# A two-layer encoder step with expert retrieval: U blocks and V blocks of the expert mixer in sequence instead of interleaved

## The chip, the cores and the metric

The kernel runs on one core of a Trainium2 chip, as one program. The metric is the device time of that core in microseconds, the median of several runs. Five engines work at once and wait for one another by semaphores: TensorE (PE in the profile), VectorE (DVE), ScalarE (ACT), GpSimd (POOL) and SyncE (SP). SP, ACT and POOL issue DMAs, each on a queue of its own.

## What is computed

One inference step of two layers over 320 tokens (256 prompt rows, 64 sample rows) of width 1024: a token mixer, cross-attention into 256 memory rows, and an expert-retrieval channel mixer, each behind an RMS norm. The change is in the expert mixer, which each of the two layers runs once:

```
q   = (xb @ w_q)                                     # 8 heads, 2 halves of 128
s   = einsum('thpc,hpnc->thpn', q, sub_keys)         # scores against 128 keys a half
...                                                  # top 16 of each half, then of the 256 sums
gate = softmax(top)                                  # 16 chosen experts a head and token
act = gelu(einsum('td,thkd->thk', xb, expert_u[eidx]))
out = einsum('thk,thkd->td', gate * act, expert_v[eidx])
```

There are 16384 experts of width 1024 for u and for v, in float32.

## The kernel before

For the 256 prompt rows the mixer is computed densely: each of 128 **U blocks** multiplies all tokens with 128 experts' u and takes the gelu; a matrix of gate weights, zero for what was not chosen, is multiplied in; each of 128 **V blocks** adds the weighted activations times 128 experts' v into four PSUM banks. For the 64 sample rows the activations come from the same U blocks and go to DRAM (`acts`), and then 64 gathered values and 64 gathered rows of v are accumulated on VectorE (`gather_step`).

All matmul operands are split into a high and a low part (float32r), and three products stand for one.

- **U block** (`split_block`): four quarters. ScalarE makes the high part of a quarter from the raw chunk (`upper_u`, line 1213), GpSimd the low part (`lower_parts`, line 629), TensorE runs 24 matmuls of 320 columns (lines 740 to 742). A quarter's buffer is free again when TensorE has used it. ScalarE takes the gelu (lines 1247, 1248). SP loads chunks of two U blocks, 1 MB, into two buffers; the load of a chunk waits until GpSimd has lowered the chunk before the last.
- **V block** (`v_block`, line 948): VectorE multiplies activations and gate weights (`product`, line 1805), ScalarE makes the high parts of p (line 1310) and v (line 1317), VectorE the low parts (lines 1814, 1816), TensorE runs 12 matmuls of 512 columns. p and v parts have two buffers each; the high parts of block b wait for block b-2. SP loads chunks of two V blocks, 1 MB, into two raw buffers (`v_load`), and the gate weights of 8 blocks, 1 MB, per round (`g_load`).
- **Gathers** (`gather_row`, `gather_act`): GpSimd issues 64 indirect row loads of 0.5 MB and 64 of single values per layer, once all U blocks are lowered. Six row slots.

Order in one layer of the mixer: queries and scores; 32 U blocks (`up`) while VectorE chooses experts; 16 U blocks beside the making of the gate matrix (`gb`), which goes to DRAM; 16 U blocks alone (`ux`); 64 rounds of one U and one V block (`uv`), the V blocks 64 blocks behind; 64 V blocks alone, into which the 64 gathered rows are accumulated. Every engine's program is written out by hand, so the order on a queue is that of the code.

## Time and profile before

| | |
|---|---|
| median of 3 runs | 2702.13 us (2697.93 to 2704.52) |
| the profiled execution | 2692.74 us, span 2690.9 us, mean granted clock of TensorE 0.963 |
| PE busy | 2454.7 us, 91% of the span |
| PE weight loads, DVE, ACT, POOL busy | 2196.0, 1447.4, 1291.1, 1421.7 us |
| HBM read and written | 459.93 and 49.68 MB |
| stages of layer 0 | `up` to 637, `gb` to 737, `ux` to 800, `uv` to 1199, V alone to 1453 us |

Matmuls are pipelined, so TensorE counts as busy while one that has been issued is still on its way; the step from the start of one block to the start of the next tells more than its busy time. Releasers are inferred from semaphores: an idle time is put down to what ended last.

### The profile page before, as it was taken

How to read it: one execution, taken by the hardware profiler on the slowest of the kernel's cores; microseconds unless marked ns; L12 is line 12 of the kernel's file. 1: busy time of each engine (PE TensorE's matmuls, PEld its weight loads, DVE VectorE, ACT ScalarE, POOL GpSimd, SP SyncE). 2: the span in 40 equal slices, each digit the busy share in tenths (PEclk: the TensorE clock that was granted, in tenths of full speed). 3: DMA queues.
4: the chain of work that ended last, by engine and by line, in shares of the span. 5: the costliest groups of instructions: out<-in, count | busy, mean ns of one | idle time of the engine just before them, and what ended most of it. 6: DMA issues, size and time to landing. Idle time of an engine off the chain costs nothing.

```text
span 2690.9 us, 48230 instructions
## 1 busy us (share of the span) xinstructions
PE 2454.7 (91%) x15014; PEld 2196.0 (82%) x15014; DVE 1447.4 (54%) x3071; ACT 1291.1 (48%) x2983; POOL 1421.7 (53%) x1772
## 2 busy tenths in 40 slices
PE   7988899998999999997778899998999999998786
PEld 7877888997999999985556878997999999985564
DVE  2233644898803333337778643898803333337787
ACT  4333534455755555543333434455855555543333
POOL 6634045786584444457721035687675444447731
PEclk9998999999999999999889999999999999999898
DMA  5313423344865564567897422243865555557794
GB/s 189 122 71 134 180 79 110 112 148 145 290 227 192 180 221 176 189 214 254 283 330 284 158 93 103 88 157 131 287 234 187 203 194 186 200 184 263 271 350 175
DMA packets 152660, 510.90 MB, mean 190 GB/s; under 512 B 13601, under 2 KB 89377, under 8 KB 110830
## 3 DMA queue, kind: packets, MB, share of 16 engines
q1 hardware_dynamic: 111662, 383.21, 40.8%
q0 software_dynamic: 31680, 118.06, 11.8%
q10 hardware_dynamic: 9216, 8.39, 0.9%
q8 instruction: 50, 0.82, 0.1%
q14 instruction: 52, 0.43, 0.0%
HBM read 459.93 MB, written 49.68 MB: 189 GB/s over the span
## 4 chain that ended last, share of the span: by engine, by line
PE 56%; POOL 19%; issue 11%; DVE 6%; DMA 5%; ACT 2%; POOLq 1%; DVEq 0%; ACTq 0%; SPq 0%
PE psum L948 14%; POOL w_split L629 12%; PE psum L740 9%; PE psum L741 9%; PE psum L742 9%; PE psum L770 9%; POOL cst L664 5%; DMA w_ring<-peer_v 3%; PE psum L996 2%; POOL w_ring L658 1%; PE psum L932 1%; DVE v_hl L1816 1%; POOL arena L658 1%; DMA w_ring<-peer_v,cst 1%; DVE arena L1376 1%
## 5 line engine op out<-in xcount | busy, mean ns | idle before, releaser
L629 POOL TENSOR_TENSOR w_split<-w_ring,w_split 128x256 fp32r<-128x256 f32 x1152 | 881.4, 771 | 590.5 <-ACT w_split L1213 498.2
L948 PE MATMUL psum<-v_hl,p_hl 128*128 128x512 f32 x3072 | 777.5, 404 | 102.2 <-DVE v_hl L1816 97.8
L740 PE MATMUL psum<-uT_split,w_split 128*128 128x320 f32 x2560 | 813.6, 318 | 20.9 <-POOL w_split L629 8.7
L742 PE MATMUL psum<-uT_split,w_split 128*128 128x320 f32 x2560 | 795.9, 311 | 0.0
L741 PE MATMUL psum<-uT_split,w_split 128*128 128x320 f32 x2560 | 795.8, 311 | 0.0
L948 PEld LDWEIGHTS psum<-v_hl,p_hl 128*128 128x128 f32 x3072 | 582.9, 194 | 260.8 <-issue 145.2
L1213 ACT ACTIVATE w_split<-w_ring 128x256 fp32r<-128x256 f32 x1152 | 480.1, 418 | 652.3 <-PE psum L742 635.8
L740 PEld LDWEIGHTS psum<-uT_split,w_split 128*128 128x128 f32 x2560 | 485.1, 190 | 43.9 <-POOL w_split L629 20.1
L741 PEld LDWEIGHTS psum<-uT_split,w_split 128*128 128x128 f32 x2560 | 485.5, 190 | 4.9
L742 PEld LDWEIGHTS psum<-uT_split,w_split 128*128 128x128 f32 x2560 | 484.8, 189 | 0.0
L1814 DVE TENSOR_TENSOR p_hl<-shared,p_hl 128x256 fp32r<-128x256 f32 x256 | 109.0, 426 | 515.0 <-ACT p_hl L1310 515.0
L1816 DVE TENSOR_TENSOR v_hl<-w_ring,v_hl 128x1024 fp32r<-128x1024 f32 x256 | 314.7, 1229 | 99.2 <-ACT v_hl L1317 98.8
L1107 ACT ACTIVATE w_split<-w_ring 128x256 fp32r (+1 forms) x416 | 171.8, 417 | 269.1 <-PE psum L770 198.5
L424 POOL TENSOR_TENSOR w_split<-w_ring,w_split 128x256 fp32r<-128x256 f32 x296 | 220.6, 750 | 151.6 <-ACT w_split L1107 139.1
L770 PE MATMUL psum<-w_split,uT_split 128*128 128x256 f32 (+1 forms) x2208 | 274.1, 287 | 18.4 <-DVE w_split L424 5.2
L770 PEld LDWEIGHTS psum<-w_split,uT_split 128*128 128x128 f32 (+1 forms) x2208 | 270.4, 183 | 22.5 <-POOL w_split L424 5.8
L1317 ACT ACTIVATE v_hl<-w_ring 128x1024 fp32r<-128x1024 f32 x256 | 268.8, 1050 | 37.0 <-DMA w_ring<-peer_v 36.9
L1310 ACT ACTIVATE p_hl<-shared 128x256 fp32r<-128x256 f32 x256 | 107.2, 419 | 294.0 <-DVE shared L1805 238.5
L1805 DVE TENSOR_TENSOR shared<-arena 128x256 f32<-128x256 f32 (+1 forms) x256 | 108.1, 422 | 112.5 <-issue 112.5
L664 POOL DMA_INDIRECT cst<-acts,cst x128 | 143.8, 1123 | 44.5 <-issue 38.4
L658 POOL DMA_INDIRECT w_ring<-peer_v,cst x84 | 86.4, 1029 | 108.7 <-DVE psum L1735 95.0
L1735 DVE SCALAR_TENSOR_TENSOR psum<-w_ring,cst,psum 128x1024 f32<-128x1024 f32 x84 | 107.7, 1282 | 26.6 <-DMA w_ring<-peer_v,cst 25.8
(260 smaller groups left out, 1874.0 us busy)
## 6 DMA issues: line engine op xcount, KB each, us to landing
w_ring<-peer_u SPq DMA_DIRECT2D x128, 1024.0 KB, 5.0
w_ring<-peer_v SPq DMA_DIRECT2D x128, 1024.0 KB, 6.1
arena<-gates SPq DMA_DIRECT2D x32, 1024.0 KB, 9.8
gates<-w_ring POOLq DMA_DIRECT2D x22, 1024.0 KB, 5.8
w_ring<-w_pq SPq DMA_DIRECT2D x8, 2048.0 KB, 7.7
gates<-arena POOLq DMA_DIRECT2D x10, 1024.0 KB, 8.5
w_ring<-w_qk SPq DMA_DIRECT2D x4, 2048.0 KB, 9.7
w_ring<-w_vo SPq DMA_DIRECT2D x4, 2048.0 KB, 7.9
```

Source lines behind the costliest of these rows:

```text
L424: eng.tensor_tensor(dst, raw, chunk_quarter(name, local, i, q, 0)[1].bitcast(F32), ALU.subtract).then_inc(w_lo_ready, 1)
L629: pool.tensor_tensor(wq[:, q, 1], quarter(raw, m, q), wq[:, q, 0].bitcast(F32), ALU.subtract).then_inc(w_lo_ready, 1)
L664: pool.indirect_dma_start(out=s_val[:, k:k + 1], out_offset=None, in_=acts[l].rearrange("a p (x o) -> (a p x) o", o=1), in_offset=bass.Ind ...
L740: pe.matmul(bank[:, 0:TOK], hi, uT_hi[:, k, :], start=k == 0, stop=False)
L741: pe.matmul(bank[:, 0:TOK], hi, uT_lo[:, k, :], start=False, stop=False)
L742: last = pe.matmul(bank[:, 0:TOK], lo, uT_hi[:, k, :], start=False, stop=k == KD - 1)
L770: last = pe.matmul(out, lhs, rhs, start=r == 0 and a == 0, stop=k == KD - 1 and a == 2, skip_group_check=True)
L948: last = pe.matmul(psum[:, 2 + 2 * t + n, :], lhs, vh[:, part, n * 512:(n + 1) * 512], start=False, stop=False, skip_group_check=True)
L1107: act.activation(dst, raw, ACT.Copy).then_inc(w_hi_ready, 1)
L1213: act.activation(wq[:, q, 0], quarter(raw, m, q), ACT.Copy).then_inc(w_hi_ready, 1)
L1317: act.activation(vhl[:, r % 2, 0, :], v_raw[(r // 2) % 2][:, r % 2, :], ACT.Copy).then_inc(vhi_ready, 1)
L1816: dve.tensor_tensor(vhl[:, r % 2, 1, :], v_raw[(r // 2) % 2][:, r % 2, :], vhl[:, r % 2, 0, :].bitcast(F32), ALU.subtract).then_inc(v_spli ...
```

## The change

All 80 late U blocks now run in one stage (`ur`), and all 128 V blocks after them. The names: EARLY = 48 blocks keep their activations in SBUF, LATE = 80 blocks do not.

- In the `ur` stage VectorE multiplies activations and gate weights in place (`weigh`): one late block at a time in `s_act`, and two early blocks beside each of the first four blocks of rounds 0 to 5. ScalarE stores the weighed late activations by groups of 4 blocks (0.5 MB) to a new DRAM tensor `weighed`, beside the samples' activations.
- SP loads 16 gate chunks in this stage, two of them into a third ring buffer by turns; three gate chunks and the first two V chunks are issued together at the stage's start.
- In the V stage the parts of v have three buffers; the third lies where the U operand was. SP reloads the weighed late activations by 8 blocks (two loads of 0.5 MB).
- The gathered rows have nine slots and are accumulated over blocks 14 to 125, and not over the last 58.
- The memset that clears rows of `u` for the next layer stands behind the wait for the last V block instead of ahead of the copies of the accumulator.

```diff
...
-LAG = 64
+AHEAD = 32
 GB = 16
-XU = 16
-AHEAD = LAG - GB - XU
-UV = (NB - LAG) // 8
+EARLY = AHEAD + GB
+LATE = NB - EARLY
+ROUNDS = LATE // 8
+CATCH = EARLY // 8
 GC = 16
 NGC = NP_ // GC
 PICKS = 64
-SLOTS = 6
+SLOTS = 9
...
-        act4 = view(arena, 0, LAG // 4, 4, NP_)
-        act8 = view(arena, 0, LAG // 8, 8, NP_)
-        g_ring = view(arena, LAG * NP_, 2, NGC, 8 * GC)
-        s_act = view(arena, LAG * NP_ + 4096, 2, 4, NS)
-        spare_rows = LAG * NP_ + 4096 + 512
-        g_stage.append(view(arena, spare_rows, NK // 2, GC, 2))
-        row_slot = [view(arena, spare_rows + h * D, D) for h in range(2)]
-        row_slot += [view(w_ring, s * KD * 512 + h * D, D) for s in range(2) for h in range(2)]
+        act4 = view(arena, 0, EARLY // 4, 4, NP_)
+        p_early = view(arena, 0, EARLY, NP_)
+        g_ring = view(arena, EARLY * NP_, 3, NGC, 8 * GC)
+        g_blocks = g_ring.rearrange("p s c (b t d) -> p s c b t d", t=GC, d=2)
+        p_late = view(arena, EARLY * NP_, 3, 8, NP_)
+        s_act = view(arena, EARLY * NP_ + 6144, 2, 4, TOK)
+        spare_cols = EARLY * NP_ + 6144 + 8 * TOK
+        g_stage.append(view(arena, spare_cols, NK // 2, GC, 2))
+        row_slot = [view(w_ring, s * KD * 512 + h * D, D) for s in range(2) for h in range(2)]
+        row_slot += [arena[:, at:at + D] for at in (16384, 18432, 19456, spare_cols, spare_cols + D)]
...
-        vhl = view(v_hl, 0, 2, 2, D)
-        pf = view(shared, 9 * P + 3 * NP_, 2, NP_)
+        vhl = [view(v_hl, 0, 2, D), view(v_hl, 2 * D, 2, D), view(uT_split, 0, 2, D)]
...
+                def u_load(c):
+                    sp.wait_ge(w_lo_ready, ubase + 8 * (c - 1))
+                    sp.dma_start(Ublk[c % 2], U[c]).then_inc(w_loaded[c % 2], 16)
+                def g_load(buffer, g):
+                    sp.dma_start(g_ring[:, buffer], g_dram[l][:, :, g].rearrange("c j x -> j c x")).then_inc(g_loaded[buffer], 16)
+                def p_load(k):
+                    for h in range(2):
+                        sp.dma_start(p_late[:, k % 2, 4 * h:4 * h + 4, :], p_dram[l][2 * k + h].rearrange("p (b t) -> p b t", t=NP_)
+                                     ).then_inc(p_loaded[k % 2], 16)
+                first = EARLY // 2
+                for c in range(first, first + 2):
+                    u_load(c)
+                for b in range(3):
+                    sp.wait_ge(g_stored[b], 16 * STAGE_USES[b] * (l + 1))
+                g_load(0, CATCH)
+                g_load(2, 0)
+                g_load(1, CATCH + 1)
+                for b in range(2):
+                    sp.dma_start(v_raw[b], V[b]).then_inc(v_loaded[b], 16)
+                for j in range(ROUNDS):
                     for q in range(4):
+                        c = first + 2 + 4 * j + q
+                        if c < NB // 2:
+                            u_load(c)
+                        if q == 0 and 1 <= j < ROUNDS - 1:
+                            sp.wait_ge(late_made, LATE * l + 8 * j)
+                            g_load((j + 1) % 2, CATCH + j + 1)
+                        if q == 2 and j + 1 < CATCH:
+                            sp.wait_ge(early_made, EARLY * l + 8 * (j + 1))
+                            g_load(2, j + 1)
+                for c in range(2, NB // 2):
+                    sp.wait_ge(v_split, NB * l + 2 * c - 2)
+                    sp.dma_start(v_raw[c % 2], V[c]).then_inc(v_loaded[c % 2], 16)
+                    k = (c - 2) // 4 - (CATCH - 1)
+                    if c == 4:
+                        sp.wait_ge(late_made, LATE * (l + 1))
+                        sp.wait_ge(weighed_stored, 16 * (LATE // 4) * (l + 1))
+                        p_load(0)
+                        p_load(1)
+                    if c % 4 == 2 and 2 <= k < ROUNDS:
+                        sp.wait_ge(p_split, NB * l + 8 * (CATCH + k - 1))
+                        p_load(k)
...
                 for k in range(SLOTS):
+                    if k == 4:
+                        pool.wait_ge(acts_stored, 16 * (NB // 4) * (l + 1))
+                        pool.wait_ge(weighed_stored, 16 * (LATE // 4) * (l + 1))
+                        pool.wait_ge(early_made, EARLY * (l + 1))
...
-                with pe.Fori(0, XU // 4) as i:
+                with pe.Fori(0, LATE // 4) as i:
                     for r in range(4):
-                        pe.wait_ge(a_emptied, i * 4 + (AJ[f"ux{l}"] + r - 1))
-                        split_block(i, 4, split_base(l, HP + LAG - XU + r), psum[:, r % 2, :])
-                with pe.Fori(0, UV) as i:
-                    for r in range(8):
-                        pe.wait_ge(a_emptied, i * 8 + (AJ[f"uv{l}"] + r - 1))
-                        split_block(i, 8, split_base(l, HP + LAG + r), psum[:, r % 2, :])
+                        split_block(i, 4, split_base(l, HP + EARLY + r), a_bank(AJ[f"ur{l}"] + r, i, 4))
+                with pe.Fori(0, NB // 6) as i:
+                    for r in range(6):
                         v_block(l, i, r)
-                with pe.Fori(UV, 16) as i:
-                    for r in range(8):
-                        v_block(l, i, r)
-                pe.wait_ge(a_emptied, AJ[f"uv{l}"] + NB - LAG)
+                for b in range(NB // 6 * 6, NB):
+                    v_block(l, NB // 6, b % 6)
...
+                def store_group(group, buffer, made):
+                    act.wait_ge(late_made, made)
+                    act.dma_start(acts[l][EARLY // 4 + group].rearrange("p (b t) -> p b t", t=NS), s_act[:, buffer, :, NP_:TOK]
+                                  ).then_inc(acts_stored, 16)
+                    act.dma_start(p_dram[l][group].rearrange("p (b t) -> p b t", t=NP_), s_act[:, buffer, :, 0:NP_]
+                                  ).then_inc(weighed_stored, 16)
+                def late_round(i, last=False):
                     for r in range(8):
+                        n, buffer, group = AJ[f"ur{l}"] + r, r // 4, r // 4
                         if not (last and r == 7):
+                            upper_u(i, 8, r + 1, EARLY, n, 8)
                         act.wait_ge(a_filled, i * 8 + (n + 1))
                         if r % 4 == 0:
+                            act.wait_ge(acts_stored, i * 32 + 16 * (first_group + EARLY // 4 + group - 1))
+                            if not (isinstance(i, int) and i == 0):
+                                act.wait_ge(weighed_stored, i * 32 + 16 * (LATE // 4 * l + group - 1))
+                        act.activation(s_act[:, buffer, r % 4, :], psum[:, ABANKS[n % 4], 0:TOK], ACT.Gelu).then_inc(a_emptied, 1)
+                        if isinstance(i, int) and i == 0 and r == 0:
+                            store_samples(EARLY // 4 - 1, 1, AJ[f"gb{l}"] + 5 * (GB - 1) + U_JOB + 1)
+                        if r % 4 == 2 and not (isinstance(i, int) and i == 0 and r == 2):
+                            store_group(i * 2 + (group - 1), 1 - buffer, i * 8 + (LATE * l + 4 * (r // 4)))
+                late_round(0)
+                with act.Fori(1, ROUNDS - 1) as i:
+                    late_round(i)
+                late_round(ROUNDS - 1, last=True)
+                store_group(LATE // 4 - 1, 1, LATE * (l + 1))
+                def p_high(b):
+                    if b < EARLY:
+                        act.wait_ge(early_made, EARLY * l + b + 1)
+                    elif b % 8 == 0:
+                        k = (b - EARLY) // 8
+                        act.wait_ge(p_loaded[k % 2], 32 * (ROUNDS // 2 * l + k // 2 + 1))
+                    act.wait_ge(v_summed, (NB + 2) * l + b + 1)
+                    act.activation(phl[:, b % 2, 0:NP_], p_block(b), ACT.Copy).then_inc(p_hi_ready, 1)
+                def vhi(b):
+                    if b % 2 == 0:
+                        act.wait_ge(v_loaded[(b // 2) % 2], 16 * (32 * l + b // 4 + 1))
+                    act.wait_ge(v_summed, (NB + 2) * l + max(b, 2))
+                    act.activation(vhl[b % 3][:, 0, :], v_raw[(b // 2) % 2][:, b % 2, :], ACT.Copy).then_inc(vhi_ready, 1)
+                vhi(0)
+                for b in range(NB):
+                    p_high(b)
+                    if b + 1 < NB:
+                        vhi(b + 1)
...
+                def weigh(act_block, buffer, r):
+                    halves_of = act_block.rearrange("p (c t) -> p c t", t=GC)
+                    return dve.tensor_tensor(halves_of, halves_of, g_blocks[:, buffer, :, r // 2, :, r % 2], ALU.mult)
+                for j in range(ROUNDS):
+                    dve.wait_ge(g_loaded[j % 2], 16 * (ROUNDS // 2 * l + j // 2 + 1))
                     for r in range(8):
+                        dve.wait_ge(a_emptied, AJ[f"ur{l}"] + 8 * j + r + 1)
+                        weigh(s_act[:, r // 4, r % 4, 0:NP_], j % 2, r).then_inc(late_made, 1)
+                        if j < CATCH and r < 4:
+                            if r == 0:
+                                dve.wait_ge(g_loaded[2], 16 * (CATCH * l + j + 1))
+                            for e in (2 * r, 2 * r + 1):
+                                weigh(p_early[:, 8 * j + e, :], 2, e).then_inc(early_made, 1)
+                def p_low(b):
+                    ph = phl[:, b % 2, :]
+                    dve.wait_ge(p_hi_ready, NB * l + b + 1)
+                    dve.tensor_tensor(ph[:, NP_:2 * NP_], p_block(b), ph[:, 0:NP_].bitcast(F32), ALU.subtract).then_inc(p_split, 1)
+                def v_low(b):
+                    dve.wait_ge(vhi_ready, NB * l + b + 1)
+                    dve.tensor_tensor(vhl[b % 3][:, 1, :], v_raw[(b // 2) % 2][:, b % 2, :], vhl[b % 3][:, 0, :].bitcast(F32), ALU.subtract
+                                      ).then_inc(v_split, 1)
+                v_low(0)
+                for b in range(NB):
+                    p_low(b)
                     if b + 1 < NB:
+                        v_low(b + 1)
+                    for k in steps_at(b):
                         gather_step(l, k)
-                if l == 0:
-                    dve.memset(u[NS:P, 2, :], 0.0).then_inc(prefix_clear, 1)
                 dve.wait_ge(rows_used, PICKS * (l + 1))
                 for n in range(2):
                     dve.tensor_copy(acc_tmp[:, n, :], psum[:, 6 + n, :]).then_inc(acc_copied, 1)
                 dve.wait_ge(v_summed, (NB + 2) * (l + 1))
+                if l == 0:
+                    dve.memset(u[NS:P, 2, :], 0.0).then_inc(prefix_clear, 1)
...
```

How instructions stand on the engines, at the places of interest:

SP's queue around the wait for the gate stores, before: gate chunks are `gates`, U and V chunks `peer_u` and `peer_v`.

```order
L502 DMA w_ring<-peer_u 128x2048
L530 DMA w_ring<-peer_v 128x2048 [waits g_stored0]
L533 DMA arena<-gates 128x16x128 [waits g_stored2,g_stored1]
L534 DMA w_ring<-peer_v 128x2048
L537 DMA w_ring<-peer_u 128x2048 [waits w_lo_ready] x2
L539 DMA arena<-gates 128x16x128 [waits g_loaded]
L507 DMA w_ring<-peer_u 128x2048 [waits w_lo_ready]
L512 DMA w_ring<-peer_v 128x2048 [waits v_split]
```

The same place on SP's queue in the change; `w_lo_ready` counts lowered quarters of U, `late_made` and `early_made` weighed blocks.

```order
L518 DMA w_ring<-peer_u 128x2048 [waits w_lo_ready] x2
L521 DMA arena<-gates 128x16x128 [waits g_stored2,g_stored1,g_stored0]
L521 DMA arena<-gates 128x16x128 x2
L538 DMA w_ring<-peer_v 128x2048 x2
L518 DMA w_ring<-peer_u 128x2048 [waits w_lo_ready] x3
L521 DMA arena<-gates 128x16x128 [waits early_made]
L518 DMA w_ring<-peer_u 128x2048 [waits w_lo_ready] x2
L521 DMA arena<-gates 128x16x128 [waits late_made]
```

Before, the wait for the gate stores came after the loads for 64 U blocks, and three loads stood between it and the next U chunk; now it comes after those for 52, and five loads stand there.

VectorE in the V-alone stage, before (p low, v low, the next product, a gathered row).

```order
L1814 TENSOR_TENSOR p_hl<-shared,p_hl 128x256 [waits p_hi_ready,p_made]
L1816 TENSOR_TENSOR v_hl<-w_ring,v_hl 128x1024 [waits vhi_ready]
L1805 TENSOR_TENSOR shared<-arena 128x256 [waits a_emptied]
L1735 SCALAR_TENSOR_TENSOR psum<-w_ring,cst,psum 128x1024 [waits rows_used,rows_gathered5]
L1814 TENSOR_TENSOR p_hl<-shared,p_hl 128x256 [waits p_hi_ready,p_made]
```

VectorE in the V stage of the change, at a gathered row; `uT_split` is the third buffer.

```order
L1840 TENSOR_TENSOR p_hl<-arena,p_hl 128x256 [waits p_hi_ready]
L1845 TENSOR_TENSOR uT_split<-w_ring,uT_split 128x1024 [waits vhi_ready]
L1755 SCALAR_TENSOR_TENSOR psum<-arena,cst,psum 128x1024 [waits rows_used,rows_gathered5]
L1840 TENSOR_TENSOR p_hl<-arena,p_hl 128x256 [waits p_hi_ready]
L1845 TENSOR_TENSOR v_hl<-w_ring,v_hl 128x1024 [waits vhi_ready]
```

The product is gone, the v low part is that of the next block and no longer of the same one, and a gathered row stands behind about every second block.

ScalarE where the U stage ends and the V stage begins, in the change.

```order
L1329 ACTIVATE arena<-psum 128x320 [waits a_filled]
L1314 DMA acts<-arena 512x1x64 [waits late_made]
L1316 DMA weighed<-arena 512x1x256
L1356 ACTIVATE v_hl<-w_ring 128x1024 [waits v_summed,v_loaded0]
L1349 ACTIVATE p_hl<-arena 128x256 [waits v_summed,early_made]
```

Before, the first high parts of p and v stood in the middle of a round, ahead of the next U block's quarters.

## Rows read from the trace of the kernel before

**Rows 1.** Stages: window, busy us (instructions) by engine, granted clock, DMA share, GB/s.
```profile
800.00:1199.00 399.00, 397.88 (x2286) 366.05 (x2284) 128.22 (x194) 211.16 (x506) 192.94 (x258) 1.00 0.54 190
1199.00:1453.00 254.00, 203.47 (x768) 150.19 (x768) 197.28 (x259) 87.08 (x126) 134.18 (x123) 0.92 0.81 286
...
2417.00:2671.00 254.00, 203.52 (x772) 150.10 (x772) 200.89 (x263) 87.37 (x127) 135.92 (x123) 0.93 0.80 283
```
**Rows 2.** Timeline of PE, interleaved stage: start us, length us, instruction, count.
```profile
1000.92 2.91 PE L948 MATMUL psum<-v_hl,p_hl 128*128 128x512 f32 x12
1003.66 0.30 PE L740 MATMUL psum<-uT_split,w_split 128*128 128x320 f32 x1
...
1007.18 2.91 PE L948 MATMUL psum<-v_hl,p_hl 128*128 128x512 f32 x12
```
**Rows 3.** Timelines of ACT and DVE, start of the V-alone stage.
```profile
1202.28 0.42 ACT L1310 ACTIVATE p_hl<-shared 128x256 fp32r<-128x256 f32 x1 [1.63 <-DVE shared L1805]
1202.61 1.05 ACT L1317 ACTIVATE v_hl<-w_ring 128x1024 fp32r<-128x1024 f32 x1
1205.29 0.42 ACT L1310 ACTIVATE p_hl<-shared 128x256 fp32r<-128x256 f32 x1 [1.64 <-DVE shared L1805]
...
1203.68 1.23 DVE L1816 TENSOR_TENSOR v_hl<-w_ring,v_hl 128x1024 fp32r<-128x1024 f32 x1 [0.46 <-ACT v_hl L1317]
```
**Rows 4.** Groups by line, 1199 to 1453 us: busy us, mean ns, idle before, releaser.
```profile
L664 POOL DMA_INDIRECT cst<-acts,cst x64 | 71.7, 1120 | 21.8 <-issue 19.2 <-DMA acts<-arena 2.6
...
L1735 DVE SCALAR_TENSOR_TENSOR psum<-w_ring,cst,psum 128x1024 f32<-128x1024 f32 x42 | 53.8, 1281 | 11.9 <-DMA w_ring<-peer_v,cst 11.5
...
L1814 DVE TENSOR_TENSOR p_hl<-shared,p_hl 128x256 fp32r<-128x256 f32 x63 | 26.3, 417 | 8.2 <-ACT p_hl L1310 8.2
```
**Rows 5.** Timeline of PE, V-alone stage, with the idle time ahead in brackets.
```profile
1230.47 7.09 PE L948 MATMUL psum<-v_hl,p_hl 128*128 128x512 f32 x24 [7.45 <-DVE v_hl L1816]
```
**Rows 6.** Timeline of SP's queue, end of the `ux` stage: issue time, length.
```profile
779.94 0.34 SPq L530 DMA_DIRECT2D w_ring<-peer_v  x1
780.38 0.41 SPq L533 DMA_DIRECT2D arena<-gates  x1
780.84 6.01 SPq L534 DMA_DIRECT2D w_ring<-peer_v  x1
786.90 6.76 SPq L537 DMA_DIRECT2D w_ring<-peer_u  x2
```
**Rows 7.** The four issues of rows 6, us to landing; last, 30 U loads alone.
```profile
w_ring<-peer_v SPq DMA_DIRECT2D x1, 1024.0 KB, 6.9
...
arena<-gates SPq DMA_DIRECT2D x1, 1024.0 KB, 10.0
...
w_ring<-peer_v SPq DMA_DIRECT2D x1, 1024.0 KB, 12.3
...
w_ring<-peer_u SPq DMA_DIRECT2D x1, 1024.0 KB, 8.7
...
DMA to landing us min/median/max: 4.7/5.0/5.1
```
**Rows 8.** Start of `ux`: POOL's last gate store, its landing, ACT's fifth U block.
```profile
737.61 0.53 POOL L642 DMA_DIRECT2D gates<-w_ring  x1 [4.94 <-ACT w_ring L1289]
...
gates<-w_ring POOLq DMA_DIRECT2D x1, 1024.0 KB, 5.8
...
750.70 0.42 ACT L1213 ACTIVATE w_split<-w_ring 128x256 fp32r<-128x256 f32 x1
```
**Rows 9.** POOL's lowering at 559 to 580, all engines at 600 to 620, POOL near 800.
```profile
L629 POOL TENSOR_TENSOR w_split<-w_ring,w_split x24: 737/746/757, 559.3 to 579.6; 128x256 fp32r<-128x256 f32 x24
...
600.00:620.00 20.00, 18.48 (x112) 16.15 (x111) 19.76 (x17) 9.64 (x29) 19.89 (x18) 1.00 0.46 159
...
796.20 5.56 POOL L629 TENSOR_TENSOR w_split<-w_ring,w_split 128x256 fp32r<-128x256 f32 x6 [2.89 <-ACT w_split L1213]
```
**Rows 10.** V loads issued in the V-alone stage of layer 0, us to landing.
```profile
DMA to landing us min/median/max: 4.8/7.3/16.0
```

153 lines of the change are left out of this document (31 added, 122 removed).

## The prediction

> **What bounds the kernel now.** I read the times by stage first, then the timelines of single engines in the two stages that the change rebuilds, then the landing times of the loads. Each layer ends with the expert mixer: 128 U blocks (u·expert_u, then gelu) and 128 V blocks (weighted sum of expert_v). At present the last 64 U blocks run interleaved with the first 64 V blocks, and the last 64 V blocks run alone. In the interleaved stretch TensorE is busy for 397.9 of 399 us at full clock; in the V-alone stretch for 203.5 of 254 us, with a granted clock of 0.92 on average, and the second layer repeats it [rows 1]. The unit costs stand in the interleaved stretch: a V block begins at 1000.92, the next U block at 1003.66, the next V block at 1007.18 [rows 2]. So on a TensorE that never waits a V block costs 2.74 us and a U block 3.52 us. The V-alone stretch takes 254.0 us for 64 blocks, 3.97 each; at 2.74 it would take 175.4. **78.6 us a layer** are lost there, and that is all there is to win.
>
> Two things lose them. Before the first gathered row is added, blocks follow each other every 3.0 us: the high part of p starts at 1202.28 and again at 1205.29, and between them stand the high part of v on ScalarE, 1.05 us from 1202.61, and its low part on VectorE, 1.23 us from 1203.68 [rows 3]. With two v buffers that chain starts when block b-2 ends and must be done before block b starts; the 0.26 us over 2.74 are its excess. The other 0.97 us a block are the 64 gathered rows, 1.28 us each on VectorE [rows 4], which stand in front of the next v low part and themselves wait for DMA: the first makes TensorE wait 7.45 us [rows 5].
>
> **The change, part by part, per layer.**
>
> *V pace.* All 128 V blocks now run alone, with a third v buffer (the U operand's space) and the 64 gathered rows spread over blocks 14 to 125. The chain of 3.0 us gets a whole block of slack. VectorE has p low 0.42, v low 1.23 and 64/112 of 1.28, that is 0.73: 2.38 us in 2.74 [rows 3, 4]. ScalarE has 0.42 and 1.05. The product with the gate weights is no longer there. So V runs at TensorE's pace if its loads come: gain 78.6.
>
> *V loads.* There are still only two raw buffers of 1 MB, and each now has to turn round in four blocks, 10.96 us. After landing come two v high parts of 1.05, a p high part of 0.42 between them, the second v low part of 1.23 and half a gathered row, together 4.3 us, so a load may take 6.6 us. A load alone lands after 5.0 us and a queued one 2.5 to 2.8 us behind the one ahead of it (786.8, 790.4, 793.1, 795.6 [rows 6, 7]), so 1 MB occupies the queue for about 2.6 us and a gathered row of 0.5 MB for half of that: 6.3 us with one gathered row in the way. In 10 rounds the reloaded p (1 MB per 8 blocks) stands ahead of one V load and adds about 1 us. I take 5 us; the bounds are 0 and 18 (every load at the 7.3 us of the V-alone stretch now [rows 10]: 11.6 us for four blocks, 2.90 a block, times 114).
>
> *U alone.* 80 U blocks run back to back; they have the same 24 matmuls each, 3.52 us [rows 2]. Three things are new.
>
> First, **a burst on SP's queue** as this stage begins. SP waits for all gate stores; the last goes out at 737.61 and lands 5.8 us later, at 743.4 [rows 8]. Then it issues three gate loads and two V loads, 5 MB, ahead of the third U chunk. The queue serves in order: the V load, gate load, V load and U load issued from 779.94 to 786.90 land one behind the other, the gate load 3.6 us after its predecessor [rows 6, 7]. From 743.5: first gate load alone at 749.4 (5.0 plus the 1.0 that a gate load is dearer), then 753.0, 756.6, 759.2, 761.8, and the U chunk at 764.4. ScalarE starts on the first block of that chunk at 750.70 [rows 8]. It will be 13.7 us late; of that about 1 is slack in the four quarter buffers. After such an idle time TensorE restarts at the lower clock: behind the wait of 7.45 us, 24 matmuls took 7.09 us where two blocks of the chain take 6.0 [rows 5]. Cost 12.7 + 1.8 = 14.5 (10 if the stores land early, 18 if U needs longer to get into step). Today the same loads stand under V work and cost nothing.
>
> Second, **weighing on VectorE beside GpSimd's lowering**. Lowering an undisturbed quarter takes 0.746 us; while VectorE ran long operations on two SBUF tiles, 18 quarters filled 20 us and TensorE issued only 112 matmuls in them; and with the p and v parts of the first V block beside them six quarters took 5.56 us [rows 9]. These are 1.1 us lost on 2.0 us of VectorE. A weighing (0.42) then costs GpSimd 0.24. Blocks with three of them (one late, two early; four in each of rounds 0 to 5, round 0 falling into the burst) need 4 x 0.75 + 0.72 = 3.7 us instead of 3.52: 20 blocks, 3 us; the others 3.4, hidden.
>
> The Trainium skill (SBUF — State Buffer, "Who interferes with whom") says more: a VectorE instruction with two SBUF inputs and a GpSimd instruction that reads SBUF exclude each other for the whole instruction. By that, such a block would need 3.0 + 1.26 = 4.2 us and the 20 blocks 14 us. The rows agree that they collide, but show about half of the full exclusion.
>
> Third, **spilling**: 20 groups of 0.5 MB of weighed p and 0.13 MB of samples leave on ScalarE's queue, 1.6 us of transfer each by the 2.6 us per MB. A U load has little room: it lands after 5.0 us and is due after some 5.4, with the 1 us of slack behind. The store goes out about half a period after a U load. I take 4 us in all; bounds 0, and 20 for 1 us at each.
>
> *Between U and V.* Nothing covers the first V block: gelu, weighing, two DMA issues, v high, v low and p low are in line. With gelu taken like a p high part, weighing like a p low part and an issue like SP's 0.34 [rows 3, 4, 6], that is 0.42 + 0.42 + 0.7 + 1.05 + 1.23 + 0.42, and handovers: 5 us (4 to 8). The samples' first row needs 9 row and 16 value gathers, about 1.1 us each and 0.3 between [rows 4], some 35 us after the stores, against 14 blocks x 2.74 = 38 us: no stall, up to 4 if it slips. The memset of 64 x 1024 that moves behind the last V block is less than half as dear as a gathered row: 0.5.
>
> Sum per layer: 78.6 - 5 - 14.5 - 3 - 4 - 5 - 0.5 = **46.6**, both layers 93. The profiled execution (2692.7, its span 2690.9) would come to 2600. It lies 9.4 below the median of the runs, so for the median 2702.1 - 93 = **2609 us**. With each term at its better end the gain is 128 (2574); with V loads, spill and lock at their worse ends it is about 13.
>
> **Rivals.** (a) *V loads land as late as now*, 7.3 us: 2.90 a block, 13 us more a layer: 2636. For it: at 286 GB/s the DMA engines were 0.81 busy [rows 1], and V, p and rows together ask for 2.1 + 0.5 + 1.2 MB in 10.96 us, 348 GB/s. Against it: the gate loads that now delay V loads are gone from this stage.
>
> (b) *Full exclusion of weighing and lowering*: 11 us more a layer, 2631. The rows speak for half.
>
> (c) *The third buffer changes nothing* because VectorE, 87% loaded, becomes the chain again: 3.0 a block, 128 x 0.26 = 33 less 5 already counted, 28 a layer: 2666.
>
> (d) *Slower: V is bound by the landing time.* Hiding V's loads under U work was what the interleaving did. The gain is gone when V loses 51.6 us over 114 blocks, at 3.19 a block, 12.8 us per four blocks: a landing time of 8.5 us. At 9 us it is 3.33 a block and 62 us more a layer: 2733. For it: single loads took up to 16 us now [rows 10]. Against it: those stood behind gate loads, and the median was 7.3 with more gathered rows per microsecond than the changed kernel has.
>
> **How the numbers follow.** Forecast 0.60, (a) 0.15, (b) 0.05, (c) 0.07, (d) 0.13, of which 0.04 ends within 0.3% of the present time (8 us, about what a measurement can tell from no change) and 0.09 above. Faster 0.87, same 0.04, slower 0.09. The range takes in the forecast's own ends but for its very best, (a), (b) and half of (c): 2568 to 2665. It leaves out (d), the rest of (c) and about 0.03 below.
>
> **What would show it.** In the changed profile: V blocks 2.74 to 2.8 us apart; VectorE's gathered rows without idle time on DMA; one idle time of TensorE of 12 to 14 us per layer, about 12 us into the U-alone stage, ended by a peer_u load; U blocks 3.52 us apart otherwise; about 5 us idle between U and V. Wrong, if the idle time before v high parts on the peer_v load is more than 20 us a layer, if lowering takes over 0.9 us a quarter in the first 48 late blocks, or if V blocks stand 3.0 us apart without such waits.

## The result, and the profile after

The changed kernel takes 2625.7 us (median of four runs, 2609.3 to 2630.3) beside 2703.3 for the kernel before on the same chip: a ratio of 0.970, interval 0.965 to 0.975. The forecast was 2609, the range 2568 to 2665. The profiled execution of the changed kernel took 2621.7 us, 71.0 less than that of before, where the sum had 93. Of the experiment e3_norow below, six of ten runs were slow, the profiled one too: its median and ratio are those of the other four, its stage times those of a slow run.

By stage, from windows of the trace (columns: window, its length, busy us and instructions of PE, PE weight load, DVE, ACT and POOL, granted clock, DMA share, GB/s); the rows are U alone and V alone of layer 0, then of layer 1:

```profile
737.80:1039.00 301.20, 283.49 (x1921) 282.96 (x1921) 85.80 (x131) 159.30 (x401) 241.71 (x323) 0.97 0.78 245
1039.00:1420.80 381.80, 360.23 (x1536) 289.17 (x1536) 275.35 (x324) 173.26 (x252) 155.09 (x124) 0.99 0.78 288
1930.80:2232.80 302.00, 284.22 (x1921) 283.70 (x1921) 83.37 (x131) 158.94 (x401) 242.98 (x323) 0.98 0.78 245
2232.80:2598.80 366.00, 354.59 (x1537) 288.10 (x1537) 276.47 (x324) 174.60 (x252) 155.00 (x124) 1.00 0.80 297
```

They answer to [rows 1]: the 80 late U blocks and all V blocks, with the four matmuls that clear V's PSUM banks ahead of them, took 715.8 us in layer 0 before and take 684.5 now (713.0 and 669.5 in layer 1). The sum put U alone, with the switch to V, at 80 x 3.52 + 26.5 = 308.1 us and V at 128 x 2.74 + 5 = 355.7. So U is 6 to 7 us better than forecast in each layer, V is 26 and 10 us worse. Between the layers, from the last V block to the U stage of layer 1, another 5.5 us went (508.4 against 502.9), of which the sum had 0.5.

V at its undisturbed pace, near the end of the stage, where no row is fetched any more (timeline of PE; the third buffer is `uT_split`):

```profile
1382.66 5.60 PE L967 MATMUL psum<-v_hl,p_hl 128*128 128x512 f32 x24
1388.10 2.88 PE L967 MATMUL psum<-uT_split,p_hl 128*128 128x512 f32 x12
```

Two blocks begin at 1382.66 and the next at 1388.10: 2.72 us each, so 128 blocks are 348.2 us. What a V stage takes above that is called its loss: 33.6 and 17.8 us. The waits in front of it (V stage of layer 0; us in total, times, longest):

```profile
ACT v_hl L1356 <- DMA w_ring<-peer_v: 54.9, 25, 6.8
DVE v_hl L1845 <- ACT v_hl L1356: 45.1, 43, 3.6
ACT uT_split L1356 <- DMA w_ring<-peer_v: 25.1, 12, 3.9
```

The high part of v waited 37 times for its load, 80 us in all; the whole loss of the stage, 33.6 us, is less than half of that.

### The profile page after: what moved, and what is told of

It is laid out like the page before. It is cut to its first block, busy times and chain, and to the rows that moved or that the text cites. A ratio compares the mean times of both kernels' runs of the same rounds, so it can differ in the third digit from the quotient of the medians.

```text
span 2619.9 us, 46124 instructions
## 1 busy us (share of the span) xinstructions
PE 2421.3 (92%) x15014; PEld 2193.4 (84%) x15014; DVE 1512.9 (58%) x3071; ACT 1290.3 (49%) x2823; POOL 1462.8 (56%) x1772
## 3 DMA queue, kind: packets, MB, share of 16 engines
q0 software_dynamic: 31680, 118.06, 11.9%
## 4 chain that ended last, share of the span: by engine, by line
PE 57%; issue 11%; POOL 10%; DMA 9%; DVE 8%; ACT 4%; POOLq 0%; ACTq 0%; another core or an unknown queue 0%; DVEq 0%; SPq 0%
PE psum L967 12%; PE psum L759 10%; POOL w_split L645 10%; PE psum L761 10%; PE psum L760 10%; PE psum L789 9%; DMA w_ring<-peer_v 8%; PE psum L1015 2%; DVE v_hl L1845 1%; ACT v_hl L1356 1%; DVE psum L1755 1%; PE psum L951 1%; DVE uT_split L1845 1%; DVE arena L1396 1%; DVE arena L1608 1%
## 5 line engine op out<-in xcount | busy, mean ns | idle before, releaser
L967 PE MATMUL psum<-v_hl,p_hl 128*128 128x512 f32 x2064 | 494.1, 394 | 34.2 <-DVE p_hl L1840 26.7
L967 PEld LDWEIGHTS psum<-v_hl,p_hl 128*128 128x128 f32 x2064 | 388.7, 189 | 127.0 <-DVE p_hl L1840 37.1
L1822 DVE TENSOR_TENSOR arena<-arena 128x256 f32<-128x256 f32 x256 | 165.9, 678 | 438.4 <-ACT arena L1329 395.4
L1845 DVE TENSOR_TENSOR v_hl<-w_ring,v_hl 128x1024 fp32r<-128x1024 f32 x172 | 210.4, 1223 | 101.4 <-ACT v_hl L1356 91.8
L967 PE MATMUL psum<-uT_split,p_hl 128*128 128x512 f32 x1008 | 244.6, 391 | 8.9 <-DVE p_hl L1840 8.2
L1349 ACT ACTIVATE p_hl<-arena 128x256 fp32r<-128x256 f32 x256 | 106.2, 415 | 265.6 <-PE psum L967 242.5
L967 PEld LDWEIGHTS psum<-uT_split,p_hl 128*128 128x128 f32 x1008 | 188.6, 188 | 53.5 <-DVE p_hl L1840 13.2
L1356 ACT ACTIVATE v_hl<-w_ring 128x1024 fp32r<-128x1024 f32 x172 | 180.4, 1049 | 88.8 <-DMA w_ring<-peer_v 84.7
L674 POOL DMA_INDIRECT arena<-peer_v,cst x70 | 95.1, 1358 | 166.8 <-DVE psum L1755 138.8
```

Source lines behind the costliest of these rows:

```text
L967: last = pe.matmul(psum[:, 2 + 2 * t + n, :], lhs, vh[:, part, n * 512:(n + 1) * 512], start=False, stop=False, skip_group_check=True)
L1356: act.activation(vhl[b % 3][:, 0, :], v_raw[(b // 2) % 2][:, b % 2, :], ACT.Copy).then_inc(vhi_ready, 1)
L1822: return dve.tensor_tensor(halves_of, halves_of, g_blocks[:, buffer, :, r // 2, :, r % 2], ALU.mult)
L1845: dve.tensor_tensor(vhl[b % 3][:, 1, :], v_raw[(b // 2) % 2][:, b % 2, :], vhl[b % 3][:, 0, :].bitcast(F32), ALU.subtract).then_inc(v_spli ...
```

## The experiments

All are edits of the changed kernel. Stage times come from windows of each kernel's profiled execution; the loss is the V stage less 348.2 us. The kernel before was timed beside each (medians of 2702 to 2713 us), so the ratios are to be compared and not the medians. The same V stage, with its code unchanged, lost 33.6 and 17.8 us in the changed kernel, and 30.4 and 32.0 in e1_burst: each is read from one execution, executions of one kernel differ by 5 to 21 us, and a difference of some 10 us in one stage says little by itself.

| | edit | median us | ratio to before, interval | V stages us | loss us |
|---|---|---|---|---|---|
| the change | | 2625.7 | 0.970 (0.965 to 0.975) | 381.8, 366.0 | 33.6, 17.8 |
| e1_burst | burst taken apart | 2605.6 | 0.961 (0.958 to 0.964) | 378.6, 380.2 | 30.4, 32.0 |
| e2_vbuf3 | third raw V buffer | 2601.3 | 0.960 (0.957 to 0.963) | 364.2, 362.7 | 16.0, 14.5 |
| e3_norow | rows left out | 2675.9 | 0.987 (0.982 to 0.991) | 410.1, 419.2 | 61.9, 71.0 |
| e4_nop | reload left out | 2599.2 | 0.960 (0.956 to 0.963) | 369.9, 359.5 | 21.7, 11.3 |
| e5_vhl2 | two buffers for v parts | 2742.2 | 1.013 (1.011 to 1.016) | 433.4, 434.1 | 85.2, 85.9 |
| e6_norow_paced | rows left out, paced | 2593.8 | 0.959 (0.957 to 0.962) | 357.1, 365.3 | 8.9, 17.1 |
| e7_noact | values left out | 2606.9 | 0.962 (0.959 to 0.964) | 371.9, 366.8 | 23.7, 18.6 |
| e9_prefill | first V parts earlier | 2613.9 | 0.966 (0.963 to 0.969) | 381.4, 371.0 | 33.2, 22.8 |
| e8_best | four edits | 2574.4 | 0.952 (0.949 to 0.954) | 361.7, 360.1 | 13.5, 11.9 |
| e10_spread | e8, values spread | 2560.2 | 0.943 (0.941 to 0.945) | 357.1, 362.1 | 8.9, 13.9 |
| e11_late | e10, values and rows later | 2538.0 | 0.937 (0.934 to 0.939) | 349.2, 349.1 | 1.0, 0.9 |
| e12_two | e11, two raw V buffers | 2573.0 | 0.951 (0.948 to 0.953) | 378.1, 367.3 | 29.9, 19.1 |

### The burst on SP's queue (e1_burst)

```diff
                 g_load(0, CATCH)
-                g_load(2, 0)
-                g_load(1, CATCH + 1)
-                for b in range(2):
-                    sp.dma_start(v_raw[b], V[b]).then_inc(v_loaded[b], 16)
...
                             u_load(c)
+                        if j == 0 and q == 0:
+                            g_load(2, 0)
+                        if j == 0 and q == 1:
+                            g_load(1, CATCH + 1)
+                        if j in (7, 8) and q == 2:
+                            sp.dma_start(v_raw[j - 7], V[j - 7]).then_inc(v_loaded[j - 7], 16)
...
```

> The changed kernel with one edit on SP's queue: of the five loads issued together at the start of the U-alone stage only the first gate load stays ahead of the third U chunk; the other two gate loads follow the next U chunks, and the first two V loads move to rounds 7 and 8. Theory (a queue served in order: the U chunk stands behind 5 MB): the single idle time of 12.7 us of TensorE in each layer and the slow restart go, the U-alone stage falls from 301 to about 287 us in each layer, and the kernel takes about 27 us less than the changed one, some 2598 us. Rival (the stall comes from the weighing, which cannot begin before its gates have landed): the idle time stays near 12 us and moves at most by a block, the time stays at 2620 to 2630. In between: if the gate loads between the U chunks delay them one by one, 10 to 20 us of the 27 come.

In the changed kernel SP's queue (timeline: start, length, instruction, count) issues three gate loads, two V loads and then the third U chunk; TensorE's first row after the idle time in brackets is below it:

```profile
741.99 6.67 SPq L521 DMA_DIRECT2D arena<-gates  x3
748.69 4.01 SPq L538 DMA_DIRECT2D w_ring<-peer_v  x2
752.75 18.85 SPq L518 DMA_DIRECT2D w_ring<-peer_u  x3
...
764.80 0.64 PE L759 MATMUL psum<-uT_split,w_split 128*128 128x320 f32 x1 [12.69 <-POOL w_split L645]
```

With the burst taken apart (windows, U alone of both layers):

```profile
742.00:1031.90 289.90, 282.78 (x1922) 281.62 (x1920) 91.14 (x131) 158.45 (x401) 245.23 (x324) 1.00 0.80 255
...
1916.60:2206.20 289.60, 282.44 (x1921) 281.65 (x1921) 88.05 (x131) 158.96 (x401) 244.31 (x324) 1.00 0.80 255
```

U alone went from 301.2 and 302.0 to 289.9 and 289.6, with the clock at full: 11.3 and 12.4 us, and the ratio from 0.970 to 0.961, some 24 us of the 27 forecast. The stall had its cause in the order on the queue. Waits of 0.7 and 1.1 us (0.4 and 1.5 in layer 1) are left near the start of the stage, where gate loads still go out between the U chunks.

### The loads of V (e2_vbuf3, e4_nop)

```diff
-        v_raw = [view(w_ring, s * KD * 512 + 2 * D, 2, D) for s in range(2)]
+        v_raw = [view(w_ring, at, 2, D) for at in (2 * D, KD * 512 + 2 * D, 0)]
...
-                    sp.wait_ge(v_split, NB * l + 2 * c - 2)
-                    sp.dma_start(v_raw[c % 2], V[c]).then_inc(v_loaded[c % 2], 16)
+                    if c == 2:
+                        sp.wait_ge(w_lo_ready, split_base(l, HP + NB))
+                    else:
+                        sp.wait_ge(v_split, NB * l + 2 * c - 4)
+                    sp.dma_start(v_raw[c % 3], V[c]).then_inc(v_loaded[c % 3], 16)
...
```

> The changed kernel with three raw V buffers in place of two (the third where the U chunks lay), and eight row slots in place of nine. In the changed kernel the V stage takes 381.8 and 366.0 us for 128 blocks that need 2.72 us each, 348. Theory (turn-round of two buffers: a load is issued only when its buffer is free and then has 6.6 us): with a third buffer each load may take some 12 us, the V stages fall to 352 to 358 us and the kernel to about 2590 us. Rival (the 16 DMA engines have no more to give while V, reloaded p and gathered rows run together): the V stages stay within 5 us of 382 and 366, the time at 2615 to 2630.

The third raw buffer costs one row slot. It took 17.6 and 3.3 us off the V stages, less than forecast, and left losses of 16.0 and 14.5, although ScalarE waited for no V load in either V stage any more.

```diff
-            return p_early[:, b, :] if b < EARLY else p_late[:, (b - EARLY) // 8 % 2, b % 8, :]
+            return p_early[:, b % EARLY, :]
...
-                        p_load(0)
-                        p_load(1)
...
-                        p_load(k)
...
```

> The changed kernel with the reload of the weighed late activations left out: late V blocks use early blocks' weighed activations again (so the prompt rows of the output are other numbers); the stores stay. Theory (the reload stands ahead of one V load in four and costs about 1 us in each of ten rounds, and 2 MB of it at once near the start): the V stages lose 8 to 15 us each, the time falls to 2600 to 2610. Rival 1 (the reload is the main cause of late V loads): V stages at 350 to 355, about 2580. Rival 2 (it costs nothing, being prefetched): V stages within 3 us.

Leaving the reload out took 11.9 and 6.5 us off. That is about the size forecast for the theory; by single stages it is no more than the scatter named above, but the ratio, 0.960, is clear of the changed kernel's. Neither edit alone brings V near 348 us; something else holds it.

### Rows and single values (e3_norow, e6_norow_paced, e7_noact)

```diff
                     if k >= SLOTS:
-                        pool.wait_ge(rows_used, PICKS * l + k - SLOTS + 1)
+                        return
...
```

> The changed kernel with 55 of the 64 row gathers of each layer left out: the nine slots are filled once and used again and again, all accumulations stay (so the sample rows of the output are other numbers). Theory of the two buffers with shared engines: a V load that meets no gathered row lands in 5 us and is in time, except behind the reloaded p; the V stages fall to 352 to 360 us, the time to about 2590. Rival (V is held up by VectorE, 87% loaded, or by the reloaded p alone): V stages stay above 365.

With less to move, V became 28 and 53 us slower in the profiled execution, and the ratio rose from 0.970 to 0.987. That is the rival's side, but not for its reason. Where (windows of layer 0, same columns as above; then the timeline of PE, and what ScalarE waited for most from 1049 to 1140 us: us in total, times, longest):

```profile
1080.00:1140.00 60.00, 18.09 (x50) 12.93 (x50) 9.78 (x12) 6.47 (x10) 41.35 (x43) 0.64 0.12 35
1160.00:1440.00 280.00, 280.00 (x1237) 231.86 (x1236) 231.94 (x268) 141.06 (x206) 0.00 (x0) 1.00 0.62 221
...
1094.10 5.49 PE L967 MATMUL psum<-uT_split,p_hl 128*128 128x512 f32 x12 [3.91 <-DVE p_hl L1840]
1110.19 4.48 PE L967 MATMUL psum<-v_hl,p_hl 128*128 128x512 f32 x12 [10.60 <-DVE p_hl L1840]
1139.59 5.08 PE L967 MATMUL psum<-v_hl,p_hl 128*128 128x512 f32 x12 [24.92 <-DVE p_hl L1840]
...
ACT p_hl L1349 <- remote: 55.3, 5, 28.0
```

From 1160 on, TensorE never waits. The whole loss lies before, with the DMA engines 0.12 busy from 1080 to 1140 us and no high part of v waiting for its load, while GpSimd issues the 64 gathers of single values back to back, from 1049.7 to 1134 us: the row gathers between them had been their pacing, and it went with the rows. My edit had changed two things. The next one keeps the pacing:

```diff
                         pool.wait_ge(rows_used, PICKS * l + k - SLOTS + 1)
+                    if k >= SLOTS:
+                        return
...
```

> Leaves out 55 of the 64 row gathers of each layer, as e3_norow did, but GpSimd keeps waiting for each row's turn, so that the 64 gathers of single values keep their places over the V stage (in e3_norow they ran one behind the other for 84 us, and the long stalls of that run lie in just that stretch). Theory A (V loads land late because the 512 KB rows take the same transfer engines): no stall, both V stages near 350 us (128 blocks at 2.72 us and a few us), total 2574 to 2592 us. Theory B (the value gathers, or the reload of the weighed activations, are what delays the V loads): V stages 362 us or longer, total 2608 to 2630 us. If the 410 us stage of e3_norow comes back, its cause is the missing rows and not the train of value gathers.

Theory A came nearer in layer 0 (357.1 us, though one stall is left) and theory B in layer 1 (365.3). But besides the switch, TensorE waited for over 0.5 us only here (timeline of PE, layer 0 and layer 1):

```profile
1071.76 4.62 PE L969 MATMUL psum<-v_hl,p_hl 128*128 128x512 f32 x12 [5.11 <-issue]
...
2228.52 4.60 PE L969 MATMUL psum<-v_hl,p_hl 128*128 128x512 f32 x12 [1.99 <-issue]
...
2244.79 7.88 PE L969 MATMUL psum<-v_hl,p_hl 128*128 128x512 f32 x24 [8.23 <-DVE p_hl L1842]
```

All three lie within the one run of value gathers that is left (1054 to 1080 in layer 0; 18 gathers from 2219 to 2242 in layer 1) or right behind it. So two things make V lose time: rows that make V loads late (without them ScalarE waited three times for a V load in layer 0, 8.8 us in all and beside the train, and not at all in layer 1), and trains of value gathers, that is, runs of them issued back to back.

```diff
                 def gather_act(k):
+                    if k % 16:
+                        return
...
```

> Leaves out 60 of the 64 gathers of single values per layer (one is issued where sixteen were); rows, V loads and the reload stay. Theory (a train of value gathers on GpSimd holds ScalarE, VectorE and TensorE up, as the stalls of e3_norow and e6_norow_paced lie only in such trains): no stall of several us in the first 50 us of the V stage, V stages 10 to 20 us shorter (362 to 370 and 350 to 358), total 2590 to 2610 us. Rival (only the bytes of the rows and of the reload count; single values move hardly any): V stages within 5 us of 381.8 and 366.0, total 2616 to 2630 us.

With the values left out, the loss went from 33.6 to 23.7 in layer 0 and stayed, 18.6 against 17.8, in layer 1: by stages partly the theory, partly the rival. The total, at a ratio of 0.962 against 0.970, is in the theory's range.

### The third buffer for the parts of v (e5_vhl2)

```diff
-        vhl = [view(v_hl, 0, 2, D), view(v_hl, 2 * D, 2, D), view(uT_split, 0, 2, D)]
+        vhl = [view(v_hl, 0, 2, D), view(v_hl, 2 * D, 2, D)]
...
-                    act.wait_ge(v_summed, (NB + 2) * l + max(b, 2))
+                    act.wait_ge(v_summed, (NB + 2) * l + max(b + 1, 2))
```

> Undoes one part of the change: two buffers for the split halves of V again instead of three, all else as in the changed kernel. Theory (the third buffer is what lets a V block go at 2.72 us instead of the 3.00 us of the chain between ScalarE, VectorE and TensorE): the stretch without gathers at the end of the V stage goes at 3.0 us per block, the V stages (381.8 and 366.0 us) become 390 to 405 us, total 2645 to 2685 us. Rival (the V stage is set by the landing of its transfers, so the buffer count does not matter): pace at the end of the stage still near 2.72, total within 6 us of 2626.

It is worth far more than the 0.26 us a block that I had priced: without it V takes 433 us, 3.39 a block, beyond either forecast, and the kernel is 1.3% slower than before. Timeline of DVE, near the end:

```profile
1456.42 1.23 DVE L1845 TENSOR_TENSOR v_hl<-w_ring,v_hl 128x1024 fp32r<-128x1024 f32 x1 [1.13 <-ACT v_hl L1356]
1457.56 1.29 DVE L1755 SCALAR_TENSOR_TENSOR psum<-arena,cst,psum 128x1024 f32<-128x1024 f32 x1
1458.75 0.42 DVE L1840 TENSOR_TENSOR p_hl<-arena,p_hl 128x256 fp32r<-128x256 f32 x1
```

The row stands between the v low part and the p low part of the same block, so with two buffers its 1.29 us can come into the chain of every second block. The chain's 0.26 us and half of 1.29 would be 0.9 us a block; 0.67 were lost. The order in which VectorE's program is written needs the third buffer.

### The switch from U to V (e9_prefill)

```diff
                         if not (last and r == 7):
                             upper_u(i, 8, r + 1, EARLY, n, 8)
+                        else:
+                            vhi(0)
+                            p_high(0)
+                            vhi(1)
...
+                        if j == ROUNDS - 1 and r == 7:
+                            v_low(0)
+                            p_low(0)
                         dve.wait_ge(a_emptied, AJ[f"ur{l}"] + 8 * j + r + 1)
...
```

> The first splits of V (high halves of blocks 0 and 1, low half of block 0) and the first split of the activations stand ahead of the last GELU and the last weighing of the U stage instead of behind them. Theory: the 5.02 us in which TensorE stands at the switch from U to V shrink to about 1 us in each layer, and the first two V blocks, 8.08 and 7.06 us at a lowered clock, come down to about 5.5 us: 10 to 14 us in all, 2612 to 2616 us. Rival: V is set by its transfers, and a start that is 5 us earlier only waits later for them: 2622 to 2628 us.

First the changed kernel, then this one (timeline of PE, first V blocks of layer 0):

```profile
1039.00 8.25 PE L967 MATMUL psum<-v_hl,p_hl 128*128 128x512 f32 x24 [5.02 <-DVE p_hl L1840]
```

```profile
1034.33 5.72 PE L967 MATMUL psum<-v_hl,p_hl 128*128 128x512 f32 x24 [0.59 <-DVE v_hl L1837]
```

The idle time fell from 5.02 to 0.59 us and two blocks from 8.25 to 5.72 us. The ratio went from 0.970 to 0.966, some 9 us, near the forecast; by the intervals alone that is not clear of the noise.

### Together, and without the trains (e8_best, e10_spread, e11_late, e12_two)

e8_best is e1, e2 and e9 with the first two reloads moved from V load 4 to loads 12 and 18.

> Four edits together: the burst in front of the third late U chunk taken apart (as e1_burst), three buffers for the raw V chunks (as e2_vbuf3), the first V splits ahead of the end of U (as e9_prefill), and the first two reloads of weighed activations at the V loads 12 and 18 instead of both at load 4. If the gains add up: e1 some 24 us, e2 some 24 us, the switch 10 to 14 us, the reloads 0 to 6 us: 2556 to 2572 us. If what the earlier edits save returns as V loads that land late (the V stage is then bound by its transfers): U stages of 289 us, but V stages of 375 us or more, 2585 to 2600 us.

2574 us, between the two forecasts (the profiled execution took 2560): U alone 286.6, V 361.7 and 360.1. What V still loses has a rhythm. GpSimd's issues of value gathers, then ScalarE's p high parts and TensorE's blocks in the same microseconds (timelines; idle time in brackets):

```profile
1053.64 0.96 POOL L685 DMA_INDIRECT cst<-acts,cst  x1 [0.31 <-issue]
1054.90 1.45 POOL L685 DMA_INDIRECT cst<-acts,cst  x1 [0.30 <-issue]
...
1059.23 1.45 POOL L685 DMA_INDIRECT cst<-acts,cst  x1 [0.31 <-issue]
...
1052.91 0.42 ACT L1332 ACTIVATE p_hl<-arena 128x256 fp32r<-128x256 f32 x1 [2.91 <-PE psum L972]
1057.24 0.42 ACT L1332 ACTIVATE p_hl<-arena 128x256 fp32r<-128x256 f32 x1 [2.96 <-PE psum L972]
1061.53 0.42 ACT L1332 ACTIVATE p_hl<-arena 128x256 fp32r<-128x256 f32 x1 [2.92 <-PE psum L972]
...
1053.84 3.01 PE L972 MATMUL psum<-v_hl,p_hl 128*128 128x512 f32 x12 [1.24 <-issue]
1058.17 3.01 PE L972 MATMUL psum<-uT_split,p_hl 128*128 128x512 f32 x12 [1.31 <-DVE p_hl L1837]
```

Every third issue takes 1.45 us instead of about 0.95, and a p high part begins 0.85 to 0.9 us after its end (1056.35, 1057.24; 1060.68, 1061.53). Blocks follow each other every 4.3 us there instead of 2.72, and ScalarE waits for no V load in the whole stage. The next kernel spreads the values:

```diff
-                for k in range(16):
-                    gather_act(k)
-                fetched = 16
-                for k in range(SLOTS, PICKS):
-                    for n in range(fetched, min(fetched + 2, PICKS)):
-                        gather_act(n)
-                    fetched = min(fetched + 2, PICKS)
-                    gather_row(k)
+                turns = [(n - 2 if n < 16 else 14 + 1.6 * (n - 16), n, False) for n in range(PICKS)]
+                turns += [(15 + 1.75 * (k - SLOTS), k, True) for k in range(SLOTS, PICKS)]
+                for block, k, row in sorted(turns):
+                    if row:
+                        gather_row(k)
+                    else:
+                        pool.wait_ge(v_split, NB * l + max(1, int(block)))
+                        gather_act(k)
```

> e8_best, with the 64 value gathers of a layer spread: value n waits for V block n-2 (the first 16), the later ones for every 1.6th block, where they now go 16 in a row and then two before each row gather. Theory (the trains hold the engines up; in e8_best TensorE has idle times of 1.2 us per block only within the train of 1043 to 1069 us and small ones up to the last value gather, none after): V stages of 361.7 and 360.9 us become 350 to 355 us, 2550 to 2562 us against 2574. Rival (each value gather costs its part wherever it stands): within 4 us of e8_best.

The time fell to 2560 us, as forecast, but the V stages, 357.1 and 362.1, did not: the row gathers ahead of the first sixteen values finish late, and those values still went out in a train in both layers. Besides the switch, all idle times over 0.2 us lie in it or right behind it. So the next step adds the first row later and gives the first sixteen values room:

```diff
-FIRST_STEP = 14
+FIRST_STEP = 22
...
-                turns = [(n - 2 if n < 16 else 14 + 1.6 * (n - 16), n, False) for n in range(PICKS)]
-                turns += [(15 + 1.75 * (k - SLOTS), k, True) for k in range(SLOTS, PICKS)]
+                turns = [(7 + 0.95 * n if n < 16 else 24 + 1.4 * (n - 16), n, False) for n in range(PICKS)]
+                turns += [(23 + 1.625 * (k - SLOTS), k, True) for k in range(SLOTS, PICKS)]
```

> e10_spread, with the first gathered row added at block 22 instead of 14, and the first sixteen value gathers one per 0.95 V block from block 7 on. In e10_spread they still went out back to back from 1043 to 1067 us, since the row gathers ahead of them on GpSimd were late, and TensorE stood 1.3 us per block in that time and hardly anywhere else in the stage. Theory (the back-to-back issue is what holds the engines up): no idle time over 1 us left in the V stage, both stages 349 to 353 us instead of 357.1 and 362.8, total 2540 to 2550 us against 2560. Rival (a value gather costs its part in the first blocks whatever its pace, or rows added over fewer blocks make V loads late): 2555 to 2570 us.

Windows: U alone and V alone of layer 0, then V alone of layer 1, then the stretch in which rows, reloads and V loads come together:

```profile
736.80:1022.40 285.60, 282.75 (x1922) 281.60 (x1920) 89.87 (x130) 158.68 (x400) 240.97 (x322) 1.00 0.81 256
1022.40:1371.60 349.20, 348.69 (x1536) 288.22 (x1537) 279.74 (x325) 172.89 (x253) 131.10 (x127) 1.00 0.85 318
...
2162.60:2511.70 349.10, 348.75 (x1537) 288.26 (x1537) 279.85 (x325) 172.86 (x253) 130.11 (x127) 1.00 0.85 314
...
1240.00:1320.00 80.00, 80.00 (x354) 66.26 (x354) 68.50 (x79) 39.75 (x58) 27.24 (x26) 1.00 0.95 365
```

V goes at TensorE's pace from end to end, 2538.0 us in all, a ratio of 0.937 and a little better than expected. The edit moved the rows as well as the values; that the values were the cause is supported by e6_norow_paced, where rows are added from block 14 on and TensorE does not wait once the train and what it left behind are over. The stretch of 80 us without an idle time of TensorE has the DMA engines 0.95 busy at 365 GB/s, so bandwidth as such was not what V lacked. The last run takes the third raw buffer away again, as in e2's diff read backwards:

> e11_late with one part undone: two raw V buffers again (and nine row slots), all else the same. It tells what the landing of V loads costs once no train of value gathers is left. In e11_late both V stages take 349 us at the pace of TensorE (128 blocks at 2.72 us), with the transfer engines 0.95 busy. Theory (a load that can only be issued when the chunk before the last is split lands too late while rows and reloads go beside it, as the prediction priced it): some 20 idle times of 0.3 to 3 us per stage in front of a p low part, V stages 356 to 368 us, total 2552 to 2575 us. Rival (the trains were all of it, and two raw buffers do): stages within 3 us of 349, total 2536 to 2545 us.

The median, 2573.0, is in the theory's range. V lost 29.9 and 19.1 us again, more than forecast (in a profiled execution of 2585.7 us), and the waits name the loads (layer 0; us in total, times, longest):

```profile
ACT v_hl L1336 <- DMA w_ring<-peer_v: 58.4, 28, 3.5
ACT uT_split L1336 <- DMA w_ring<-peer_v: 20.0, 11, 3.7
```

So late loads alone can cost as much as the changed kernel lost (33.6, 17.8), where no train is left. But its own loss has two parts. Its last value gather goes out at 1203.8 us in layer 0 and at 2390.9 in layer 1. Split there, the V stages read as follows (windows of the changed kernel, both layers):

```profile
1039.00:1205.00 166.00, 157.50 (x665) 126.98 (x666) 116.64 (x138) 76.11 (x111) 106.49 (x92) 0.97 0.78 282
1205.00:1420.80 215.80, 202.72 (x873) 162.19 (x871) 158.71 (x187) 97.16 (x142) 48.59 (x33) 1.00 0.78 292
2232.80:2392.00 159.20, 152.96 (x659) 124.10 (x660) 115.50 (x136) 75.43 (x109) 110.98 (x92) 0.99 0.82 293
2392.00:2598.80 206.80, 201.63 (x880) 164.00 (x878) 160.97 (x188) 99.17 (x144) 44.01 (x32) 1.00 0.79 300
```

And of e2_vbuf3, split behind its last value gather in the same way:

```profile
1040.90:1206.00 165.10, 155.12 (x658) 123.65 (x659) 116.51 (x137) 74.28 (x109) 103.42 (x93) 0.99 0.80 282
1206.00:1405.10 199.10, 199.10 (x879) 164.61 (x878) 162.46 (x188) 97.69 (x143) 39.45 (x33) 1.00 0.84 314
2215.90:2378.00 162.10, 154.59 (x652) 125.27 (x653) 114.94 (x135) 73.71 (x109) 102.55 (x93) 0.96 0.80 285
2378.00:2578.60 200.60, 200.60 (x886) 165.85 (x884) 163.94 (x190) 98.50 (x144) 40.29 (x34) 1.00 0.83 308
```

At 2.72 us for 12 matmuls, the changed kernel lost 15 and 10 us up to the last value gather and 18 and 7 us behind it. With the third raw buffer 16 us (14 in layer 1) are lost up to the last value gather and nothing behind it. So behind it the loss is that of late loads. Up to it loads were late too (25 us of waits in layer 0), but taking these waits away brought nothing there: the value gathers hold V up as long. Neither cause alone accounts for the loss, and only e11_late, with both gone, has none. The whole third raw buffer is worth some 26 us beside the value trains (ratios 0.970 and 0.960) and 38 without them (0.951 and 0.937); the intervals do not tell the two apart.

## Why the prediction was right, and where it was off

- **What bounded the kernel before** was right. The idle time lay in the V-alone stage, and the change took about half of it away: 78.6 us a layer were to be had, and 31 and 43 us came.
- **V pace** was right: 2.72 us a block where nothing is late, against 2.74 in [rows 2]. VectorE, busy 275 of 382 us, did not become the bound: rival (c) fell. It was right for the third buffer too, though e5_vhl2 shows that I had undervalued it: I counted it as 0.26 us a block of chain and left out that the row then stands in the chain as well.
- **V loads: the step that failed.** The sum had 5 us a layer, the bounds 0 and 18; the V stages lost 33.6 and 17.8. Of that, 18 and 7 us, behind the last value gather, are late loads alone. The 15 and 10 us before came beside the value gathers, of which the prediction had asked only whether they end in time: that they hold V blocks up was priced at nothing. The step on the loads said that a load may take 6.6 us and takes 6.3 with one gathered row in the way. Three loads of the changed kernel, and the v high parts that waited for them (timelines of SP and of ACT):

```profile
1184.44 0.33 SPq L555 DMA_DIRECT2D w_ring<-peer_v  x1
1191.58 1.06 ACT L1356 ACTIVATE v_hl<-w_ring 128x1024 fp32r<-128x1024 f32 x1 [1.28 <-DMA w_ring<-peer_v]
...
1196.04 0.33 SPq L555 DMA_DIRECT2D w_ring<-peer_v  x1
1202.21 1.06 ACT L1356 ACTIVATE uT_split<-w_ring 128x1024 fp32r<-128x1024 f32 x1 [0.25 <-DMA w_ring<-peer_v]
...
1206.98 0.33 SPq L555 DMA_DIRECT2D w_ring<-peer_v  x1
1214.93 1.06 ACT L1356 ACTIVATE v_hl<-w_ring 128x1024 fp32r<-128x1024 f32 x1 [2.09 <-DMA w_ring<-peer_v]
```

  They landed after 7.1, 6.2 and 8.0 us. Taken in the same way, 36 of the 62 loads that are issued in layer 0's V stage were late, after 5.0 to 12.7 us, with a median of 7.6; in layer 1 it was 32, with a median of 7.0. I had priced a queue in which a fixed amount stands ahead of each load, and set a mean landing against a limit with 0.3 us of room. The landing was mis-sized by about 1 us, and its spread was left out: with two buffers each late load is lost, while an early one gives nothing back. Rival (a), 2.90 us a block from the 7.3 us of [rows 10], was the better price by its number, the two stages came to 2.98 and 2.86, but not by its mechanism, since part of the loss is not the loads'. The point from which V would eat the whole gain, 8.5 us (rival (d)), was passed by 13 of these loads in layer 0 and 2 in layer 1, and not by the median.
- **The burst** was right: 12.7 us forecast, 12.69 and 12.76 us measured, ended by the lowering of a chunk whose `peer_u` load ScalarE had waited for, at the place named, and e1_burst shows its cause. In detail it ran otherwise: the gate stores had landed 1.4 us earlier, and SP spent some 2 us on each issue (6.67 us for three, 4.01 for two) instead of some 0.4.
- **Weighing beside lowering** was mis-sized: 3 us forecast, none seen; behind the burst, U blocks follow each other every 3.52 us to the end of the stage. Rows of VectorE's weighing and GpSimd's lowering from 765 to 1034 us (count, ns min/median/max):

```profile
L1822 DVE TENSOR_TENSOR arena<-arena x118: 409/739/1026, 765.2 to 1031.3; 128x256 f32<-128x256 f32 x118
L645 POOL TENSOR_TENSOR w_split<-w_ring,w_split x303: 728/735/997, 764.7 to 1031.0; 128x256 fp32r<-128x256 f32 x152
```

  The two collide, but VectorE pays: a weighing takes 0.74 us instead of 0.42, a quarter's lowering 0.735 as ever. I had read the price from stretches in which VectorE ran long operations [rows 9]; beside short ones the lowering, which fills most of GpSimd's time here (241.7 of 301 us), keeps its length. VectorE has time in this stage. The Trainium skill (SBUF — State Buffer, "Who interferes with whom") says that two such instructions contend for a port pair, that the pair is an exclusive lock, and that the order of issue decides who blocks. The trace agrees as far as that the weighing's extra 0.3 us, at most 0.6, fit within one lowering of 0.735. The 14 us that I drew from the rule were laid on the wrong engine, and rival (b) fell.
- **Spilling** was mis-sized too: 4 us forecast, none seen. ScalarE waited 6.1 us in 16 times for a store of weighed blocks, and TensorE had no idle time but the burst's. The lower bound of 0 was the right end.
- **Between U and V**: 5 us forecast, 5.02 measured in both layers. Left out was that TensorE comes back at a lower clock: over the first two blocks the granted clock was 0.67 in layer 0 and 0.79 in layer 1, and they took 8.08 and 6.89 us to the next one's start where 5.44 is full pace, 2.6 and 1.5 us more. I had counted such a restart behind the burst and forgot it here.
- **Between the layers** 5.5 us were lost, not 0.5. The memset takes 0.91 us, and TensorE's first matmul behind the V stage's last sums comes 9.98 us after them instead of 9.05. For the rest I made no experiment, and it stays open.

That the time fell within the range is in part luck. The V stages cost 26 and 10 us more than the sum had, and only the 6 to 7 us that the U stages cost less stood against it; the range was wide enough because it had taken rival (a) in, and (a) covers a part of what happened.

## What to carry over

When a stage is freed of its chain and goes at TensorE's pace, the next limit is the landing of its loads: price the spread of landings, not the mean alone, and ask how many buffers stand between a late load and the engine. Where two causes of stall meet in one stage, read the loss by stretch before you judge a fix by the total: the third raw buffer took away all that was lost behind the last value gather and nothing before it. An experiment that leaves out an instruction also leaves out the pacing that its waits gave to others.

## What the runs showed that I had not expected

- **Trains of single-value gathers hold the other engines up.** When GpSimd issues them back to back, V blocks come every 4.3 us instead of 2.72 (e8_best, 1049 to 1071), and in a train of 64 TensorE stands for up to 24.92 us with the DMA engines 0.12 busy (e3_norow). Spread at one per 0.95 to 1.4 V blocks, 2.6 to 3.8 us, they cost next to nothing (e11_late). What ScalarE waits for meanwhile the profile does not show; the idle times are put down to "remote", "issue" or a TensorE block, and the cause stays open.
- **Short runs do little.** In e11_late six rows and then six values go out back to back (1033.7 to 1049.8 us), and the only idle time of TensorE behind them is 0.49 us.
- **The DMA engines carried 365 GB/s at 0.95 busy for 80 us** without one late V load, once three raw buffers took up the spread; with two, the same stretch had 330 GB/s at 0.87, and TensorE busy for 76.03 of 80 us.
